# First weight block of a feed-forward layer: product M3g after M5g and M6g, up weights in two loads, copy of M6u and the rests of T2 earlier in their queues

## The reference

```python
def swiglu(h, w_gate, w_up, w_down):
    return (jax.nn.silu(h @ w_gate) * (h @ w_up)) @ w_down
...
        h = rmsnorm(x, ffn_norm_w[layer])
        x = x + swiglu(h, w_gate[layer], w_up[layer], w_down[layer])
```

## Time and profile before

| | us |
|---|---|
| median of 3 runs | 2322.51 (2319.41 to 2324.29) |
| the profiled execution's own time | 2318.57 |
| its span (first to last instruction) | 2316.8 |
| PE busy | 2288.7 (99%) |
| PE clock granted, mean | 0.999 of full |

### The profile page before, as it was taken

One profiled execution on the slowest core, in us unless ns is written; L12 is line 12 of the kernel. 1 busy time (PEld: TensorE's weight loads), 2 busy tenths in 40 slices (PEclk: granted clock), 3 DMA queues, 4 the chain that ended last, 5 costly groups with the idle time before them and its releaser, 6 DMA issues.

```text
span 2316.8 us, 29409 instructions
## 1 busy us (share of the span) xinstructions
PE 2288.7 (99%) x10838; PEld 1870.0 (81%) x10838; DVE 1254.8 (54%) x1659; ACT 1055.9 (46%) x1898; POOL 1194.6 (52%) x841
## 2 busy tenths in 40 slices
PE   7999999999999999999999999999999999999998
PEld 6867878888888888788888888888878888888887
DVE  7457653333336777557248348338763333336777
ACT  4046543333333446465257248238553333333445
POOL 3224288777774654233224214314388777774654
PEclk9999999999999999999999999999999999999999
DMA  5100322323228744221212212113222323227744
GB/s 161 46 28 19 118 74 99 118 87 118 87 100 283 256 149 118 58 79 59 65 55 73 65 46 91 45 56 100 98 69 107 118 87 118 87 100 277 259 146 158
DMA packets 166932, 247.92 MB, mean 107 GB/s; under 512 B 18432, under 2 KB 111500, under 8 KB 164236
## 3 DMA queue, kind: packets, MB, share of 16 engines
q1 hardware_dynamic: 162172, 233.99, 30.7%
q10 hardware_dynamic: 4624, 12.06, 1.3%
HBM read 192.93 MB, written 53.08 MB: 106 GB/s over the span
## 4 chain that ended last, share of the span: by engine, by line
PE 95%; DVE 2%; DMA 1%; POOL 1%; issue 1%; ACT 1%; SPq 0%; ACTq 0%; DVEq 0%
PE ps L1458 29%; PE ps L1460 29%; PE ps L1459 29%; PE ps L1969 1%; PE ps L1961 1%; PE ps L1954 1%; PE ps L1481 1%; PE ps L1669 1%; PE ps L1934 1%; PE ps L1648 1%; PE ps L1678 1%; DMA wv_g<-in_w_gate 0%; POOL p_lo L770 0%; PE ps L1545 0%; PE ps L1635 0%
## 5 line engine op out<-in xcount | busy, mean ns | idle before, releaser
L745 POOL TENSOR_TENSOR w_lo<-w_raw,w_hi 128x1024 fp32r<-128x1024 f32 x74 | 176.7, 2392 | 381.0 <-ACT w_hi L918 333.1
L846 POOL TENSOR_TENSOR s_lo<-s_val,s_hi 128x512 fp32r<-128x512 f32 x154 | 233.7, 1519 | 202.8 <-ACT s_hi L1236 202.5
L2252 DVE TENSOR_TENSOR xres<-ps,xres 128x512 f32<-128x512 f32 x132 | 90.6, 688 | 417.3 <-PE ps L1460 401.3
L1458 PE MATMUL ps<-xn_hi,w_hi 128*128 128x512 f32 x784 | 310.1, 395 | 0.5 <-DVE qT L2457 0.5
L1459 PE MATMUL ps<-xn_lo,w_hi 128*128 128x512 f32 x784 | 305.4, 390 | 0.0
L1460 PE MATMUL ps<-xn_hi,w_lo 128*128 128x512 f32 x784 | 305.3, 389 | 0.0
L1458 PE MATMUL ps<-xn_hi,p_hi 128*128 128x512 f32 x704 | 274.6, 390 | 1.0 <-POOL p_lo L770 0.8
L1460 PE MATMUL ps<-xn_hi,p_lo 128*128 128x512 f32 x704 | 273.9, 389 | 0.0
L1459 PE MATMUL ps<-xn_lo,p_hi 128*128 128x512 f32 x704 | 273.9, 389 | 0.0
L770 POOL TENSOR_TENSOR p_lo<-p_val,p_hi 128x512 fp32r<-128x512 f32 x176 | 237.3, 1357 | 36.5 <-ACT p_hi L1050 36.5
L1050 ACT ACTIVATE p_hi<-p_val 128x512 fp32r<-128x512 f32 x176 | 111.2, 632 | 305.1 <-POOL p_val L794 305.1
(11 more groups left out here) (285 smaller groups left out, 5026.9 us busy)
## 6 DMA issues: line engine op xcount, KB each, us to landing
s_val<-hidden SPq DMA_DIRECT2D x154, 256.0 KB, 2.8
hidden<-xres SPq DMA_DIRECT2D x20, 1792.0 KB, 6.5
wv_g<-in_w_gate SPq DMA_DIRECT2D x22, 1024.0 KB, 5.3
wv_u<-in_w_up SPq DMA_DIRECT2D x22, 1024.0 KB, 5.2
w_raw<-in_ssd_w_in SPq DMA_DIRECT2D x40, 512.0 KB, 3.8
d_val<-in_w_down SPq DMA_DIRECT2D x70, 256.0 KB, 3.7
rows_v<-in_w_down SPq DMA_DIRECT2D x64, 256.0 KB, 3.7
mdec<-decay_sums SPq DMA_DIRECT2D x32, 512.0 KB, 3.8
```

What stands on the lines that cost most here:

```text
L745: pool.tensor_tensor(w_lo[piece.slot][:, :], raw[piece.raw][:, :], f(w_hi[piece.slot][:, :]), ALU.subtract).then_inc(lo_done, 1)
L846: pool.tensor_tensor(s_lo[i][:, :], s_val[i][:, :], f(s_hi[i][:, :]), ALU.subtract)\
L1458: pe.matmul(dst, l_hi, r_hi, start=first, stop=False, skip_group_check=reopened)
L2252: dve.tensor_tensor(tmp, bank, tmp, ALU.add).then_inc(c_ready, 1)
```

## The change

It does five things, all for p = 0 of each layer.

1. M3g moves behind M5g and M6g, to the sequence that all other blocks have. M5g and M3g then share bank c, the sum for block 12 is one step, and M5g waits for the release of turn 6 instead of turn 7.
2. The up weights of p = 0 are loaded by two transfers of 512 KB; ACT's rounding for M1u waits for the first only.
3. ACT copies M6u out of PSUM ahead of the rounding for M7u, instead of behind four roundings for the next block; silu of block 21 moves ahead of the rounding for the next block's M1g.
4. On ACT the rounding of T1 (quarter 3) goes ahead of that of T2 (quarter 2).
5. On DVE the computation of T3 (quarter 3) goes behind the rests of T2.

```diff
-FIRST_PAIR = ("M1g", "M2g", "M1u", "M2u", "M3g", "M5g", "M6g", "M7g", "M5u", "M6u", "M4g", "M3u", "M7u")
+FIRST_PAIR = ("M1g", "M2g", "M1u", "M2u", "M5g", "M6g", "M3g", "M7g", "M5u", "M6u", "M4g", "M3u", "M7u")
...
-        def bank_m5(p, m):
-            return ps[:, 6, :] if (p, m) == (0, "g") else bank_c(m)
...
-                    sp.dma_start(wv[m][:, :, :], w[:, p * 2 * P:(p + 1) * 2 * P].rearrange("(k p) c -> p k c", p=P))\
-                        .then_inc(wv_loaded[m], 16)
+                    cols = w[:, p * 2 * P:(p + 1) * 2 * P].rearrange("(k p) c -> p k c", p=P)
+                    if (m, p) == ("u", 0):
+                        sp.dma_start(wv[m][:, 0:H2, :], cols[:, 0:H2, :]).then_inc(wv_half, 16)
+                        sp.dma_start(wv[m][:, H2:, :], cols[:, H2:, :]).then_inc(wv_loaded[m], 16)
+                    else:
+                        sp.dma_start(wv[m][:, :, :], cols).then_inc(wv_loaded[m], 16)
...
-                    if n in (1, 2, 4):
+                    if (p, mn) == (0, "M1u"):
+                        act.wait_ge(wv_half, 16 * (layer + 1))
+                        src = v[:, 0:H2, 0:P]
+                    elif n in (1, 2, 4):
...
                 tail_first(3)
+                tail_hi1(3)
                 tail_hi2(2)
-                tail_hi1(3)
...
                 silu(0, "12")
+                copy_out(0, "M6u")
                 p_hi_of(0, "M7u")
                 silu(0, "22")
+                silu(0, "21")
                 p_hi_of(1, "M1g")
-                silu(0, "21")
                 p_hi_of(0, "M4u")
                 p_hi_of(1, "M2g")
-                copy_out(0, "M6u")
...
+                        elif mn == "M5g":
+                            turn_free(layer, 6)
+                            pe.wait_ge(comb_lo_done, comb_lo_order.count(layer, "T1", 3))
                         elif mn == "M3g":
                             pe.wait_ge(comb_lo_done, comb_lo_order.count(layer, "B22", 3))
-                            turn_free(layer, 6)
-                        elif mn == "M5g":
-                            pe.wait_ge(comb_lo_done, comb_lo_order.count(layer, "T1", 3))
-                            turn_free(layer, 7)
...
                 product(0, "M2u")
-                product(0, "M3g")
                 product(0, "M5g")
                 product(0, "M6g")
+                product(0, "M3g")
                 product(0, "M7g")
...
                 tail_lo1(3)
-                tail_t3(3)
                 tail_lo2(1)
                 tail_t4(2)
                 tail_lo2(2)
                 tail_t4(3)
                 tail_lo2(3)
+                tail_t3(3)
                 for i in range(1, 4):
                     tail_lo3(i)
...
-                    if (p, blk, m) == (0, "12", "g"):
-                        dve.wait_ge(t_copied, copy_order.count(layer, 0, "M6g"))
-                        dve.tensor_tensor(tmp_of(blk, m), bank, tmp_of(blk, m), ALU.add).then_inc(c_ready, 1)
```

More of the change, by code:

```diff
@@ L409, in trunk @@
                            + [(p, n) for p in range(1, NP) for n in ("M1g", "M5g", "M6g", "M1u", "M5u", "M6u")])
-        c_order = Order([(0, n) for n in ("11g", "11u", "half12g", "12g", "22g", "12u", "22u")]
+        c_order = Order([(0, n) for n in ("11g", "11u", "12g", "22g", "12u", "22u")]
                         + [(p, n) for p in range(1, NP) for n in ("11g", "12g", "22g", "11u", "12u", "22u")])
@@ L415, in trunk @@
         comb_val_order = Order([(n, i) for i in range(2) for n in ("T1", "T2", "T3", "T4")]
-                               + [(n, i) for i in (2, 3) for n in ("T1", "T2", "T3")] + [("T4", 2), ("T4", 3)])
+                               + [("T1", 2), ("T2", 2), ("T3", 2), ("T1", 3), ("T2", 3), ("T4", 2), ("T4", 3), ("T3", 3)])
         comb_hi_order = Order([("B11", 0), ("B21", 0), ("B11", 1), ("B21", 1), ("B11", 2), ("B21", 2), ("B12", 0), ("B22", 0),
@@ L498, in trunk @@
         comb_pool_done = sem("comb_pool_done")
+        wv_half = sem("wv_u_half_loaded")
         wv_loaded = {"g": sem("wv_g_loaded"), "u": sem("wv_u_loaded")}
@@ L776, in w_sum @@
                     if n == 5:
+                        if (m, p) == ("u", 0):
+                            pool.wait_ge(wv_half, 16 * (layer + 1))
                         pool.wait_ge(wv_loaded[m], 16 * (layer * NP + p + 1))
@@ L1138, in ffn @@
                 tail_first(3)
+                tail_hi1(3)
                 tail_hi2(2)
-                tail_hi1(3)
                 def copy_out(p, mn):
                     m, n = mn[2], int(mn[1])
-                    bank, blk = {1: (bank_a(layer, m), "11"), 5: (bank_m5(p, m), "22"),
+                    bank, blk = {1: (bank_a(layer, m), "11"), 5: (bank_c(m), "22"),
                                  6: (bank_a(layer, m), "12")}[n]
@@ L1752, in product @@
                         pe.wait_ge(t_copied, copy_order.count(layer, p, "M1" + m))
-                    elif n == 3 and (p, m) != (0, "g"):
+                    elif n == 3:
                         pe.wait_ge(t_copied, copy_order.count(layer, p, "M5" + m))
@@ L1758, in product @@
                         pe.wait_ge(c_ready, c_order.count(layer, p, "22" + m))
-                    bank = (bank_a(layer, m) if n in (1, 6, 7, 4) else bank_b(layer, m) if n == 2
-                            else bank_m5(p, m) if n == 5 else bank_c(m))
-                    starts = n in (1, 2, 5) or (p, mn) == (0, "M3g")
+                    bank = bank_a(layer, m) if n in (1, 6, 7, 4) else bank_b(layer, m) if n == 2 else bank_c(m)
+                    starts = n in (1, 2, 5)
                     t1, t2 = slice(0, BANK), slice(BANK, S)
@@ L2242, in c_block @@
                     n, c, bank = {"11": (2, 1, bank_b(layer, m)), "12": (3, 6, bank_c(m)), "22": (7, 5, bank_a(layer, m))}[blk]
-                    if (p, blk, m) == (0, "12", "g"):
-                        dve.wait_ge(t_copied, copy_order.count(layer, 0, "M6g"))
-                        dve.tensor_tensor(tmp_of(blk, m), bank, tmp_of(blk, m), ALU.add).then_inc(c_ready, 1)
-                        c_order.step(layer, 0, "half12g")
-                        dve.wait_ge(c_ready, c_order.count(layer, 0, "half12g"))
-                        n, bank = 5, bank_m5(0, "g")
                     tmp = tmp_of(blk, m)
```

## The result

The kernel with the change took 2327.55 us (median of 12 runs, 2323.24 to 2331.85), the kernel before, in the runs beside it, 2322.29 (12 runs, 2318.86 to 2324.84). The ratio is 1.0024, interval 1.0016 to 1.0031: **5.3 us slower**. Forecast were 2326.1 and a range from 2318.5 to 2329.5.

The account below looks back on a forecast made before the run. PE was taken to bound the kernel, with at most 6.9 us of waits to win. Median 2322.51 plus 1.9 us from order plus 1.7 for one clock fall gave 2326.1 us; range 2318.5 to 2329.5.

Parts of the forecast that it names:

- T4 at 1.8 in layer 0 also: DVE's T4 of quarter 1 takes about 1.8 us in layer 0 too, instead of 0.68, held up by POOL.
- M5g near 0.5: M5g waits for DVE's rest of T1 of quarter 3: bracket near 0.5, a new wait of 0.6 us.
- 3.7 us in either layer: New wait at M6g for DVE's last rest of T2, three POOL instructions each costing DVE 1.1 us; bounds 0.2 and 4.8.
- DVE keeps the port: Faster rival: DVE's five instructions before M6g run through without POOL holding them up; 2317.2 us, chance 0.12 in whole or great part.
- Taking T3 away saves 0.6: Moving T3 of quarter 3 behind the rests of T2 on DVE saves 0.6 us of M6g's wait.
- +1.9 us: Net cost of order alone, new waits less removed ones: +1.4 us in layer 1 and +0.5 in layer 0.
- one of the two waits: PE's clock falls behind one of the two M6g waits, costing 1.7 us; bounds 0 and 3.65 per fall.
- The rival of two falls: Slower rival: the clock falls behind the M6g waits of both layers, 2 x 1.7 us; 2327.8 us, chance 0.24.
- Once both waits pass about 2.7 us: Condition for clock falls in both layers: both M6g waits longer than about 2.7 us, the idle time at the kernel's end.
- 1.9 us idle left the clock alone: Ground for the clock holding: PE idle for 1.9 us at 20.30 kept the granted clock at 1.00.
- the waits at M7u were booked in full: Copy of M6u moved up removes the waits at M7u entirely: -1.94 us in layer 0, -1.28 in layer 1.
- its use is after M7u, so I cost it at nothing: ACT's rounding for the next M1g comes one or two instructions later (0.6 us each), at no cost.

Follow-up runs that it names:

- one load: The whole change with the up weights of p = 0 in one load again, against the kernel before: 2327.03 us, ratio 1.0028.
- three copies, halves: Kernel before with the copies of M6u, M1g(1) and M5g(1) moved up on ACT and the up weights in two halves: 2316.95 us, ratio 0.9980.
- POOL's sum late: The whole change, but POOL's first up sum waits for M6g instead of M5g, against the kernel before: 2327.93 us, ratio 1.0028.
- filler: The whole change plus 12 matmuls with unused result ahead of M6g's wait in the first block, against the kernel before: 2323.04 us, ratio 1.0010.
- two copies: Kernel before with the copy of M6u and silu 21 moved up, and the copy of M1g(1) ahead of the rounding for M7g(1): 2319.40 us, ratio 0.9997.
- order undone: The change with the old order of products and T3 in its old place, against the kernel before: 2320.73 us, ratio 0.9999.
- copy only: Kernel before with only the copy of M6u and silu of block 21 moved up: 2321.59 us, ratio 0.9999.
- order only: Kernel before with only M3g moved behind M6g: 2323.94 us, ratio 1.0009.
- T3 kept: The change with T3 of quarter 3 back ahead of the rests of T2, against the kernel before: 2327.40 us, ratio 1.0025.
- change, next copy up: The whole change with the copy of M1g(1) ahead of the rounding for M7g(1), against the kernel before: 2324.14 us, ratio 1.0013.

## Why the prediction was right, point by point

**M1u near 290.7**: 290.71. **T4 at 1.8 in layer 0 also**: 1.77. **M5g near 0.5**: 0.47 and 0.48. Right, and by the mechanism given; "one load" and "three copies, halves" show the two sides of this trade.

**M6g, "3.7 us in either layer"**: 3.23 + 0.16 = 3.4. The account of DVE's five instructions, three of them held up by 1.1, is what the rows show, and the run with POOL's sum late took one of the three away and with it 1.1 us. The "some 0.3 of gaps" was not there. The profile names "issue" for this wait, where I had forecast DVE's rest; that rest ended 0.10 before M6g. The rival "DVE keeps the port" fell: six of six collisions shown above, four in the change and two with the sum late, alternate. One count against it was wrong, though: of the five rests and T4s of layer 1 before, two were held up (1.32, 1.78), not three. And its ground, the row at 305.26, is real: in the change too POOL's second up sum takes 2.64 (307.58, below), beside four rests of T4 that DVE runs through without a break. What decides who goes ahead stays open.

```profile
306.59 2.48 DVE L2198 TENSOR_TENSOR t_lo<-t_val,t_hi 128x512 fp32r<-128x512 f32 x4
```

**Taking T3 away saves 0.6**: 0.5.

**Order, net "+1.9 us"**: +1.1 in the ledger, by M6g's 0.3 in each layer and a little more won at M7g and M7u. The terms were right in kind and too high by 0.8.

**The clock, "one of the two waits", 1.7 us**: price right (1.5 per fall in most, 2.5 in two), number too low. The profiled execution had exactly the case of the forecast, one fall of two, but the filler's 3.2 us say that many runs have both. The rival of two falls (2327.8) was nearer to the median of 2327.55. Two of its grounds did not hold. "Once both waits pass about 2.7 us": the clock fell behind a wait of 2.17 and held behind 3.22, 3.23 and 3.25. "1.9 us idle left the clock alone": it did in the kernel before, but behind the same idle time of 1.9 to 2.0 us at the kernel's start it fell in three of the 14 profiled executions ("two copies", "three copies, halves", "POOL's sum late").

**The step that failed**: the waits at M7u were booked in full (-1.94 and -1.28), and of what comes later for it, "its use is after M7u, so I cost it at nothing". I looked at the next M1g, the first user of the rounding, and not at the other end of the next block's chain. There is a second bound there, the chain from the load of the next gate weights over POOL's sums to the ACT copy of M1g(1), with some 0.5 us of slack in the kernel before (copy done at 335.4, M6g(1) due near 335.9). PE is 1.6 us later there with the change, but the chain is later by 2.8. These are its links:

```profile
307.58 2.64 POOL L798 TENSOR_TENSOR p_val<-p_val,wv_u 128x512 f32<-128x512 f32 x1 [5.67 <-PE ps L1467]
...
315.25 0.37 SPq L603 DMA_DIRECT2D wv_g<-in_w_gate  x1
...
321.41 0.60 ACT L1171 ACTIVATE xres<-ps 128x512 f32<-128x512 f32 x1 [1.08 <-PE ps L1467]
321.90 0.62 ACT L1057 ACTIVATE p_hi<-wv_g 128x512 fp32r<-128x512 f32 x1
...
337.60 0.58 ACT L1159 ACTIVATE xres<-ps 128x512 f32<-128x512 f32 x1
```

POOL's second up sum waits for the late M6g and starts at 307.58, not 305.26; the next gate load is issued at 315.25, not 313.42; the copy comes at 337.60, not 334.79. The load explains 1.3 of these 2.8 us: issued 1.8 later, its weights took 5.4 us to land and not 5.9, and were there at 320.7. The next 1.2 arise on ACT: the rounding of these weights runs at 321.90, because part 3 put silu of block 21 ahead of it (321.41), and that waits for PE. Before, the rounding ran as soon as the weights were there, at 319.43. In layer 1 it does so after the change too (1716.16, landed at 1716.1), so this is a loss of layer 0 alone, and no run has the silu in its old place with the rest of the change. The last 0.3 come among POOL's instructions behind it.

The next block's wait cost 1.84, and without the order it takes back what M7u had won (3.3 of 3.4 with the order undone, 4.3 of 3.4 with the copy only). Three errors stand against each other in the sum of 3.6: nothing for the next block (1.84), too little for the clock (1.7 for about 3), and 0.8 too much for the order. They left it 1.7 short of the 5.3 measured and inside the range, which is in part luck.

## What to carry to other kernels

A wait that you remove is worth what is left of it at the next place where that engine waits: follow PE's operands one block further, to their load, before you book it. When two engines share a port, count the collisions (each was 1.1 us here, where they took turns) and ask who runs beside whom after the move. A wait of 3 us on PE can cost half as much again by the clock (1.5 us per fall, 2.5 in two cases), so matmuls whose result is thrown away may pay where the wait can't be removed.

## What the runs showed that I had not expected

Two waits of the same length in the same execution (3.23 and 3.25 us) had different ends: the clock fell behind one and held behind the other. All waits of the first block's M6g over 2 us in the profiled executions, with what the clock did (its time against PE's start behind the wait):

| run | layer 0 | layer 1 |
|---|---|---|
| change | 3.23: fell, 1.3 after | 3.25: held |
| order only | 3.38: fell, 1.1 after | 3.39: fell, 1.4 before |
| T3 kept | 3.74: fell, 0.9 after | 3.73: fell, 1.5 before |
| change, one load | 2.77: fell, 0.5 before | 3.22: fell, 0.7 after |
| change, next copy up | 3.23: held | 3.22: held |
| change, POOL's sum late | 2.16: held | 2.17: fell, 1.2 after |

Of the ten waits of 2.8 to 3.7 us seven had a fall, so 1.4 of two per execution. Their lengths do not tell which. Where the clock fell 1.4 or 1.5 before PE's start it stayed down for 6.8 us, otherwise for 3.4. Order only, layer 1, with PE still idle (x0) and then at work:

```profile
1697.60:1698.90 1.30, 0.00 (x0) 0.00 (x0) 1.30 (x4) 0.77 (x2) 0.00 (x0) 0.50 0.00 0
1699.60:1704.20 4.60, 4.60 (x12) 3.54 (x11) 4.60 (x8) 0.00 (x0) 0.00 (x0) 0.50 0.00 0
```

In layer 0 of the change it fell only after the wait: the matmuls from 303.47 to 304.38 start 0.23 apart, and the seven from 304.73 on each 0.43 ahead of the next, with one step of 0.35 between.

```profile
304.15 0.39 PE L1466 MATMUL ps<-comb_lo,p_hi 128*128 128x512 f32 x1
304.38 0.56 PE L1467 MATMUL ps<-comb_hi,p_lo 128*128 128x512 f32 x1
304.73 0.63 PE L1465 MATMUL ps<-comb_hi,p_hi 128*128 128x512 f32 x1
305.16 0.63 PE L1466 MATMUL ps<-comb_lo,p_hi 128*128 128x512 f32 x1
```

So whoever looks for the clock only where PE stands still can miss it; the granted clock of the stretch behind the wait shows it.
